# A two-block transformer kernel: unit matrices added by VectorE in an RWKV scan, a store waited for later, and branch gates computed beside memory attention

## The chip, the core and the metric

The kernel is one program for one core of one Trainium2 chip. TensorE (PE) multiplies matrices into PSUM; VectorE (DVE), ScalarE (ACT) and GpSimd (POOL) work on tiles of 128 partitions; SyncE (SP) issues the transfers. Each engine takes its instructions in the order in which they are written, and engines wait for one another by semaphores. The metric is the device time of one execution in microseconds (us).

## The reference

The first block has an attention layer and a recurrent layer, the second a mixer of three branches between two feed-forward layers. Two parts matter here. In the recurrent layer, an RWKV scan goes forwards and backwards over 256 context and 512 latent tokens, eight heads of 64:

```python
def wkv_scan(s0, r, decay, k, v, kk, b, reverse, emit):
    def step(s, inp):
        r_t, w_t, k_t, v_t, kk_t, b_t = inp
        sa = jnp.einsum('bhij,bhj->bhi', s, kk_t)
        s = s * w_t[:, :, None, :] - sa[..., None] * b_t[:, :, None, :] + v_t[..., None] * k_t[:, :, None, :]
        y = jnp.einsum('bhij,bhj->bhi', s, r_t) if emit else None
        return s, y
```

In the mixer the three branches are gated and merged:

```python
        o_dn = rms_norm_2(o_dn, dn_out_norm[l]) * jax.nn.silu(dn_z.reshape(b, s, DN_HEADS, DN_HEAD_DIM))
        o_mem = memory_cross_attention(...)
        gates = jax.nn.sigmoid(u @ w_branch_gate[l]).reshape(b, s, N_BRANCH, d)
        merged = (gates[:, :, 0] * (o_nsa @ w_branch_nsa[l])
                  + gates[:, :, 1] * (o_dn @ w_branch_dn[l])
                  + gates[:, :, 2] * (o_mem @ w_branch_mem[l]))
        x = x + rms_norm_2(merged @ w_out[l], mix_post_norm[l])
```

## The kernel before, in words

The program is a chain of stages. A stage has its own tiles and semaphores, and ends when all engines have come to its end and the transfers it waits for have landed. Weights are split into a high and a low part (ACT's cast at L197, DVE's difference at L201), and a product of a 128x512 tile with eight blocks is 24 matmuls (L220 to L222).

`rwkv_features` makes decay, key and query tiles of the scan, in eight units. A unit has four 128x768 tiles for `s_feat` in device memory: two called `out` (buffers in `rec_y` and a feature tile), a rate and a key tile. SP stores them at L1970 once the semaphore `features` says that the whole unit is done, and loads the first group's tiles back (L1977) after unit 6.

`rwkv_scan` takes 64 tokens as one chunk. Twelve groups (n = 0 to 11), two directions in turn, hold two chunks of all eight heads. The state after a chunk needs the inverse of a triangular 64x64 matrix per head and chunk. It is made from diagonal blocks by powers: the inverse of 1 + D is (1 - D)(1 + D^2)(1 + D^4)(1 + D^8) and so on, so `square`, `four` and `eight` are made one from another, each multiplied onto `inv`; then two steps, `upper` (ux) and `halved` (wx), join the halves. The unit matrices in these factors come from PE: `constant` (L2291) multiplies the unit matrix `eye` with `units` or `twice` into PSUM, and the products (`tiles`, L2282) are added there. A matmul of 64 rows uses a quadrant of the array; "crossed" products take their rows and write their columns on different quadrants. The results come out of PSUM in halves: ACT copies one (`half`, L2614), DVE the other (`odd_half`, L2552). DVE also makes `diag_t`, `diag` (L2533, L2538) and the masked grams (L2547), and the state (L2570, L2571); POOL forms the first factor (L2502) and `off_t` (L2506). The scan of group n-1 (`scan_sa` L2428, `scan_new` L2447 and L2452, `scan_out` L2442 and L2468) is written between the steps of group n, by hand; eight groups with n >= 4 have output, added to `rec_scanned` (L2581, L2585).

In the mixer, the 24 gate tiles of 128x512 are u times a weight, scaled by DVE (`rooted`, L3785). Eight (`gates_first`) are made beside the delta scan (`Beside`), twelve (`gates_kept`) in the earlier attention and kept in device memory (`s_gate`), and four in the stage `merge_gates` after memory attention. There, too, the first eight sigmoids (`Opened`, L824) and the norm of the delta branch's output (`NormAside`: square L1203, sums L1185, root L1206, reciprocal L1211, spread L1193, application L1215, then the product at L3940) are placed between its tiles. `merge0`, `merge1`, `merge2` multiply a branch with its weight; DVE multiplies the result with the gate (L3948) and adds. `merge0` also holds the twelve kept tiles' sigmoids. `InPairs` puts a `Beside` product between an attention's pairs.

Of the kernel before, what the change touches and what calls it, by code (L numbers as in the profile page):

```python
# [724 lines left out]
class Beside:  # L725
# [4 lines left out]
    def __init__(self, w, name, x, lo, evict, banks):  # L730
        self.w, self.x, self.lo, self.evict, self.banks = w, x, lo, evict, banks
        self.first, self.end = w.ranges[name]
        self.limit, self.tiles = w.split_limit(name), self.end - self.first

    def begin(self, st):
        self.ps = [st.ps(f"beside{i}", [P, BANK]) for i in range(self.banks)]
        self.product_done, self.stored = st.sem("beside_product_done"), st.sem("beside_stored")
# [27 lines left out]


class InPairs:
# [10 lines left out]
    def sp(self, sp):  # L778
        for n in range(self.product.tiles):
            self.product.load(sp, n)  # L780
            sp.wait_ge(self.product.stored, n + 1)
            self.put(sp, n).then_inc(self.saved, 16)
        sp.wait_ge(self.saved, 16 * self.product.tiles)
# [6 lines left out]
    def act(self, act, i):  # L790
        if i % self.per == 0 and i // self.per < self.product.tiles:
            self.product.high(act, i // self.per)

# [9 lines left out]
class Opened:  # L803
# [4 lines left out]
    def __init__(self, tiles, per, arrived=None):  # L808
        self.tiles, self.per, self.arrived = tiles, per, arrived
# [10 lines left out]
    def act(self, act, n, wait_stored):  # L820
        if n == 0 and self.arrived is not None:
# [1097 lines left out]
def rwkv_features(nc, name, d, c, v, us, vt, v_feat, bonus, ends, spare, loads, up_w, up_a, first_feats):  # L1919
# [7 lines left out]
    with Stage(nc, name) as st:  # L1927
# [16 lines left out]
         gated, gate_done, lifted, rate_gated, rate_done, key_scale, logs, exps, keyed, kept, features, own, first) = (  # L1944
# [3 lines left out]
                 "key_scale", "logs", "exps", "keyed", "kept", "features", "own", "first"))  # L1948
# [14 lines left out]
        def _(sp):  # L1963
            sp.dma_start(sums[:], d["c_sums"]).then_inc(landed, 16)
            for n in range(n_units):
                at = slice((n % 4) * P, (n % 4) * P + P)
                sp.wait_ge(features, n + 1)
                for j, (tile, sem) in enumerate(((out[n % 2][0], saved_out[n % 2]), (out[n % 2][1], saved_out[n % 2]),
                                                 (rates[n % 3], saved_keys[n % 3]), (keys[n % 3], saved_keys[n % 3]))):
                    sp.dma_start(d["s_feat"][n // 4, j, at, :], tile).then_inc(sem, 16)  # L1970
# [10 lines left out]
            for i in range(3):  # L1981
                sp.wait_ge(saved_keys[i], 32 * len(range(i, n_units, 3)))
# [2277 lines left out]
```

## Time and profile before

| | |
|---|---|
| median of 3 runs | 3320.42 us (3320.09 to 3335.84) |
| profiled execution | 3320.01 us, its span 3318.2 us |
| PE busy | 2961.3 us, 89% |
| DVE busy | 1521.4 us, 46% |
| ACT busy | 1090.3 us, 33% |
| POOL busy | 30.2 us, 1% |
| reload of the kept gates, 3072 KB | 11.0 us from issue to landing |

The shares are means over the whole span. A matmul of four-byte data on 64 rows has two records in the trace, so 32 matmuls in the code are 64 records. PEclk is the clock granted to TensorE, 0.50 being 1.2 GHz and 1.00 being 2.4 GHz. Names in a row are those of the tiles, without buffer numbers. The program's last part is the second feed-forward layer, which the change leaves alone.

### The profile page before, as it was taken

The numbers are of one execution on the slowest core, as the hardware profiler recorded it, in microseconds if no ns is written. First come the engines' busy times: TensorE is split into PE (matmuls) and PEld (weight loads), VectorE is DVE, ScalarE is ACT, GpSimd is POOL, SyncE is SP. The second block draws the span as 40 slices with busy tenths as digits, with TensorE's granted clock in tenths as the row PEclk, the third lists the DMA queues.
The fourth block names the chain that finished last, engine by engine and source line by source line (L and its number), as shares of the span: only waits on it lengthen the run. The fifth ranks groups of instructions, "written<-read, shape, count | busy, mean of one in ns | idle before, by whom it ended". The sixth has DMA issues, their size and how long they took to land. (4 is left out here: it accounts for less than half of the span.)

```text
span 3318.2 us, 55284 instructions
## 1 busy us (share of the span) xinstructions
PE 2961.3 (89%) x24050; PEld 2254.6 (68%) x24050; DVE 1521.4 (46%) x2488; ACT 1090.3 (33%) x1929; POOL 30.2 (1%) x28
## 2 busy tenths in 40 slices
PE   7799989989986898887899999799887988899998
PEld 3488766867854777445788787566655866788876
DVE  5623247354545344556454424355446435354522
ACT  5411367232253333212322123355323233332221
POOL 0000000000000010000000000000000000000000
PEclk9899999989968999788999998899888999999998
DMA  7511200123113111111233222421212122222321
GB/s 267 151 58 51 49 1 2 51 76 127 33 74 126 42 42 42 35 64 51 64 95 95 86 88 65 129 67 42 77 51 66 33 77 70 70 77 90 97 86 64
DMA packets 246083, 243.36 MB, mean 73 GB/s; under 512 B 28248, under 2 KB 216152, under 8 KB 245777
## 3 DMA queue, kind: packets, MB, share of 16 engines
q1 hardware_dynamic: 245538, 238.64, 23.1%
q8 instruction: 190, 3.11, 0.4%
q10 hardware_dynamic: 304, 1.18, 0.1%
q14 instruction: 51, 0.42, 0.0%
HBM read 217.03 MB, written 22.24 MB: 72 GB/s over the span
## 5 line engine op out<-in xcount | busy, mean ns | idle before, releaser
L201 DVE TENSOR_TENSOR second_w_low<-second_w_raw,second_w_high 128x1024 fp32r<-128x1024 f32 (+1 forms) x228 | 272.4, 1197 | 483.0 <-ACT second_w_high L197 482.4
L197 ACT CAST second_w_high<-second_w_raw 128x1024 fp32r<-128x1024 f32 (+1 forms) x228 | 233.0, 1024 | 689.5 <-PE ffn_in_acc L222 250.9
L220 PE MATMUL ffn_in_acc<-ffn_h_high,second_w_high 128*128 128x512 f32 x704 | 281.1, 399 | 13.9 <-DVE ffn_h_low L578 13.9
L222 PE MATMUL ffn_in_acc<-ffn_h_high,second_w_low 128*128 128x512 f32 x704 | 283.0, 402 | 0.0
L221 PE MATMUL ffn_in_acc<-ffn_h_low,second_w_high 128*128 128x512 f32 x704 | 279.7, 397 | 0.0
L201 DVE TENSOR_TENSOR first_w_low<-first_w_raw,first_w_high 128x1024 fp32r<-128x1024 f32 x115 | 140.1, 1222 | 266.4 <-ACT first_w_high L197 265.7
L197 ACT CAST first_w_high<-first_w_raw 128x1024 fp32r<-128x1024 f32 x115 | 120.2, 1047 | 233.2 <-PE attn_in_acc L222 80.9
L220 PEld LDWEIGHTS ffn_in_acc<-ffn_h_high,second_w_high 128*128 128x128 f32 x704 | 133.5, 190 | 47.8 <-issue 17.1
L220 PE MATMUL attn_in_acc<-attn_h_high,first_w_high 128*128 128x256 f32 (+1 forms) x416 | 144.3, 347 | 14.4 <-DVE attn_h_low L323 14.4
L221 PEld LDWEIGHTS ffn_in_acc<-ffn_h_low,second_w_high 128*128 128x128 f32 x704 | 133.7, 190 | 34.2 <-issue 0.5
L222 PEld LDWEIGHTS ffn_in_acc<-ffn_h_high,second_w_low 128*128 128x128 f32 x704 | 133.6, 190 | 31.1
L220 PE MATMUL ffn_down_acc<-ffn_mid_high,second_w_high 128*128 128x512 f32 x352 | 141.9, 403 | 5.9 <-PEq L43 5.9
L221 PE MATMUL attn_in_acc<-attn_h_low,first_w_high 128*128 128x256 f32 (+1 forms) x416 | 142.6, 343 | 0.0
L222 PE MATMUL attn_in_acc<-attn_h_high,first_w_low 128*128 128x256 f32 (+1 forms) x416 | 142.5, 342 | 0.0
L222 PE MATMUL ffn_down_acc<-ffn_mid_high,second_w_low 128*128 128x512 f32 x352 | 140.1, 398 | 0.0
L221 PE MATMUL ffn_down_acc<-ffn_mid_low,second_w_high 128*128 128x512 f32 x352 | 139.8, 397 | 0.0
L220 PEld LDWEIGHTS attn_in_acc<-attn_h_high,first_w_high 128*128 128x128 f32 x416 | 79.4, 191 | 30.1 <-issue 15.9
L221 PEld LDWEIGHTS attn_in_acc<-attn_h_low,first_w_high 128*128 128x128 f32 x416 | 79.7, 192 | 9.7 <-issue 0.2
L222 PEld LDWEIGHTS attn_in_acc<-attn_h_high,first_w_low 128*128 128x128 f32 x416 | 79.5, 191 | 9.8
L220 PEld LDWEIGHTS ffn_down_acc<-ffn_mid_high,second_w_high 128*128 128x128 f32 x352 | 67.0, 190 | 22.2 <-issue 6.7
L222 PEld LDWEIGHTS ffn_down_acc<-ffn_mid_high,second_w_low 128*128 128x128 f32 x352 | 66.9, 190 | 16.9
L220 PE MATMUL rwkv_in_acc<-rec_h_high,first_w_high 128*128 128x512 f32 (+1 forms) x208 | 71.3, 343 | 7.2 <-PEq L43 7.2
(801 smaller groups left out, 6378.3 us busy)
## 6 DMA issues: line engine op xcount, KB each, us to landing
second_w_raw<-in_ffn_w_gate SPq DMA_DIRECT2D x44, 512.0 KB, 3.6
second_w_raw<-in_ffn_w_up SPq DMA_DIRECT2D x44, 512.0 KB, 3.6
second_w_raw<-in_ffn_w_down SPq DMA_DIRECT2D x40, 512.0 KB, 3.4
first_w_raw<-in_rec_w_in SPq DMA_DIRECT2D x33, 512.0 KB, 3.8
first_w_raw<-in_attn_ada_w SPq DMA_DIRECT2D x24, 512.0 KB, 4.7
first_w_raw<-in_rec_ada_w SPq DMA_DIRECT2D x24, 512.0 KB, 5.1
second_w_raw<-in_w_in SPq DMA_DIRECT2D x24, 512.0 KB, 3.7
second_w_raw<-in_w_branch_gate SPq DMA_DIRECT2D x24, 512.0 KB, 3.9
```

Source lines behind the costliest of these rows:

```text
L197: act.copy(self.view(self.high[b % self.splits], b), self.view(self.raw[b % self.bufs], b)).then_inc(self.high_done, 1)
L201: dve.tensor_tensor(self.view(self.low[b % self.splits], b), self.view(self.raw[b % self.bufs], b), self.view(self.high[b % self.splits], ...
L220: pe.matmul(out, sh, mh, start=(first and j == 0), stop=False)
L221: pe.matmul(out, sh, ml, start=False, stop=False)
L222: ins = pe.matmul(out, sl, mh, start=False, stop=(last and j == len(parts) - 1))
```

## The change

1. Scan. `constant` is gone. `square`'s products and the last factor's are on crossed quadrants like the rest, which needs `diag_crossed`: eight more matmuls in the early gram, and a DVE operation. DVE's `with_units` brings both halves out of PSUM and adds `units` or the new `lower` as it does. ACT's halves are gone. POOL's first factor is in two parts, and POOL clears `rec_scanned`, which DVE did. PE's first gram no longer waits for DVE.
2. Features. `out` tiles are stored when they stand (`outs`), and the last unit's rate and key stores are waited for in the scan (`last_saved`).
3. Gates. `merge_gates` is gone. Its four tiles are made beside memory attention; sigmoid becomes 0.5 (1 + tanh) with 0.5 in the scale before and in the copy after `mix_out`; the tanh of the first eight is in the delta scan, the norm in `merge0`, the tanh of kept tiles in `merge0` (from its tile 4) and `merge1`.

```diff
-        for tile in self.tiles[n * self.per:(n + 1) * self.per]:
-            act.activation(tile, tile, ACT.Sigmoid).then_inc(self.opened, 1)
+        for tile in self.tiles[(n - self.first) * self.per:(n - self.first + 1) * self.per]:
+            act.activation(tile, tile, ACT.Tanh).then_inc(self.opened, 1)
...
+                sp.wait_ge(outs, n + 1)
+                for j in range(2):
+                    sp.dma_start(d["s_feat"][n // 4, j, at, :], out[n % 2][j]).then_inc(saved_out[n % 2], 16)
                 sp.wait_ge(features, n + 1)
-                for j, (tile, sem) in enumerate(((out[n % 2][0], saved_out[n % 2]), (out[n % 2][1], saved_out[n % 2]),
-                                                 (rates[n % 3], saved_keys[n % 3]), (keys[n % 3], saved_keys[n % 3]))):
-                    sp.dma_start(d["s_feat"][n // 4, j, at, :], tile).then_inc(sem, 16)
+                for j, tile in ((2, rates[n % 3]), (3, keys[n % 3])):
+                    sp.dma_start(d["s_feat"][n // 4, j, at, :], tile
+                                 ).then_inc(saved_keys[n % 3] if n + 1 < n_units else last_saved, 16)
...
+                else:
+                    sp.wait_ge(last_saved, 32)
...
             def square(n):
                 if n:
-                    pe.wait_ge(act_done, RWKV_ACT(n - 1, "way"))
-                constant(late, 0, all_of(units), 0)
-
-                def products():
-                    pe.wait_ge(dve_done, RWKV_DVE(n, "diag"))
-                    for h in range(2):
-                        tiles(late, 0, dt, dn, 0, 0, (h,), False)
-                        tiles(late, 256, dn, dt, 0, 0, (h,), False).then_inc(pe_done, 1)
-                return products
+                    pe.wait_ge(act_done, RWKV_ACT(n - 1, "solved"))
+                pe.wait_ge(dve_done, RWKV_DVE(n, "diag"))
+                tiles(late, 0, dt, dn, 0, 1)
+                tiles(late, 256, dn, dt, 0, 1).then_inc(pe_done, 1)
...
+                pe.wait_ge(dve_done, RWKV_DVE(n, "square1"))
+                tiles(early, 0, a2[:, 1], a2[:, 0], 1, 0)
+                tiles(early, 256, a2[:, 0], a2[:, 1], 1, 0).then_inc(pe_done, 1)
+                pe.wait_ge(pool_done, RWKV_POOL(n, "first1"))
+                tiles(late, 0, a2[:, 1], m, 1, 0).then_inc(pe_done, 1)
...
             def sixteen(n):
                 pe.wait_ge(dve_done, RWKV_DVE(n, "eight"))
-                constant(early, 0, all_of(units))
                 pe.wait_ge(act_done, RWKV_ACT(n, "m2"))
-                tiles(late, 0, a8, m, 0, 0).then_inc(pe_done, 1)
...
-                constant(sa_ps, 256, wide(twice[:, 0]))
...
+            pool.memset(y[:], 0.0).then_inc(zeroed, 1)
             for n in range(last + 1):
                 dr = groups[n][0]
+                each = eye.rearrange("p (a t) -> p a t", a=1).broadcast_to([P, PAIRS, CH])
                 pool.wait_ge(dve_done, RWKV_DVE(n, "diag"))
-                pool.tensor_tensor(all_of(m).rearrange("p (a t) -> p a t", t=CH),
-                                   eye.rearrange("p (a t) -> p a t", a=1).broadcast_to([P, 2 * PAIRS, CH]),
-                                   all_of(dn).rearrange("p (a t) -> p a t", t=CH), ALU.subtract).then_inc(pool_done, 1)
+                pool.tensor_tensor(m[:, 0], each, dn[:, 0], ALU.subtract).then_inc(pool_done, 1)
...
-            dve.memset(state[:], 0.0).then_inc(cleared, 1)
-            dve.memset(y[:], 0.0).then_inc(cleared, 1)
+            for dr in range(2):
+                dve.tensor_tensor(near[:, dr, :], chunk[:, 2 * dr, :], same, ALU.mult)
...
+                of = bank(out_ps, 1)[:, 256:512].rearrange("p (i t) -> p i t", t=CH)
+                dve.tensor_tensor(crossed[:], of, mask(1 - dr), ALU.mult).then_inc(dve_done, 1)
...
-            def odd_half(n, name, to, ps):
+            def with_units(n, name, to, ps, of=units):
                 dve.wait_ge(pe_done, RWKV_PE(n, name))
-                dve.tensor_copy(to[:, :, 1].rearrange("p a i t -> p a (i t)"),
-                                bank(ps, 1).rearrange("p (a t) -> p a t", a=2)).then_inc(dve_done, 1)
+                for h in range(2):
+                    dve.tensor_tensor(to[:, :, h].rearrange("p a i t -> p a (i t)"),
+                                      bank(ps, h).rearrange("p (a t) -> p a t", a=2),
+                                      of.rearrange("p a i t -> p a (i t)"), ALU.add).then_inc(dve_done, 1)
...
+                    with_units(n, "square", a2, late)
...
-                    odd_half(n, "ux", ux, early)
-                    odd_half(n, "wx", wx, sa_ps)
+                    with_units(n, "ux", ux, early)
+                    with_units(n, "wx", wx, sa_ps, lower)
...
+                    if n:
+                        beside.treat(act, n - 1)
+                beside.treat(act, 7)
...
+            attention(nc, "mem", pairs, [dict(out=branch[2][:, :, t * P:(t + 1) * P]) for t in range(4)], c["ident"], dims=P,
+                      beside=InPairs(Beside(w, "gates_last", *u, lambda e, n, ps: rooted(e, last_tile(n), ps, 0.5), 1, last_tile), 2))
...
-            linear(nc, "merge_gates", w, *u, S, lambda e, n, ps: rooted(e, gate(done + n), ps), engines="v",
-                   then=lambda n: lambda act: act.activation(gate(done + n), gate(done + n), ACT.Sigmoid),
...
+            norm_out = NormAside(c, "dn_out", [branch[1][:, i, :] for i in range(4)], [v("dn_out_norm")] * 4,
+                                 c["pick_mean128"], spread[0:4, :], rs[0:4, :], [out[:, 5, :], out[:, 6, :]], normed,
+                                 dict(square=lambda i: i // 2, sum=lambda i: 1 + i // 2, root=3, inverse=3, apply=lambda i: 5 + i // 2),
+                                 finish=lambda dve, i: dve.tensor_tensor(branch[1][:, i, :], branch[1][:, i, :],
+                                                                         zg[:, i, :], ALU.mult))
+            asides = [Asides(norm_out, Opened([gate(GATES_FIRST + i) for i in range(8)], 2, kept, 4)),
+                      Asides(Opened([gate(GATES_FIRST + i) for i in range(8, GATES_KEPT)], 2)), None]
...
-                ins = dve.tensor_tensor(g, g, ps[:, 0:S], ALU.mult)
+                ins = dve.scalar_tensor_tensor(out=g, in0=g, scalar=1.0, in1=ps[:, 0:S], op0=ALU.add, op1=ALU.mult)
```

PE's queue in the scan, from the early gram of group 1 (`rwkv_early`, `rwkv_out`) to the first product of the fours, before:

```order
L2306 MATMUL rwkv_early<-rwkv_feat 64x128 x16
L2324 MATMUL rwkv_out<-rwkv_feat 64x64 x16
L2291 MATMUL rwkv_late<-rwkv_units,rec_chunk 64x512 x4
L2282 MATMUL rwkv_late<-rwkv_diag,rwkv_diag_t 64x64 x8
L2282 MATMUL rwkv_late<-rwkv_diag_t,rwkv_diag 64x64 x8
L2282 MATMUL rwkv_late<-rwkv_diag,rwkv_diag_t 64x64 x8
L2282 MATMUL rwkv_late<-rwkv_diag_t,rwkv_diag 64x64 x8
L2428 MATMUL rwkv_sa<-rwkv_state,rwkv_way 64x64 x8
L2291 MATMUL rwkv_early<-rwkv_twice,rec_chunk 64x256 x4
L2282 MATMUL rwkv_early<-rwkv_square 64x64 x32
```

and after:

```order
L2312 MATMUL rwkv_early<-rwkv_feat 64x128 x16
L2328 MATMUL rwkv_out<-rwkv_feat 64x64 x16
L2333 MATMUL rwkv_out<-rwkv_feat 64x64 x8
L2297 MATMUL rwkv_late<-rwkv_diag,rwkv_diag_t 64x64 x16
L2297 MATMUL rwkv_late<-rwkv_diag_t,rwkv_diag 64x64 x16
L2426 MATMUL rwkv_sa<-rwkv_state,rwkv_way 64x64 x8
L2297 MATMUL rwkv_early<-rwkv_square 64x64 x32
```

The constants are out, the squares are two sets instead of four, and a set of eight is added to the gram.

DVE's queue in the scan, from `upper` of one group to `four` of the next, before:

```order
L2552 COPY rwkv_upper<-rwkv_early 128x2x256
L2552 COPY rwkv_halved<-rwkv_sa 128x2x256
L2547 TENSOR_TENSOR rwkv_gram_k<-rwkv_early,rec_chunk 128x512 x2
L2533 TENSOR_TENSOR rwkv_diag_t<-rwkv_early,rwkv_near 128x256 x2
L2538 TENSOR_TENSOR rwkv_diag<-rwkv_out,rwkv_near 128x256 x2
L2547 TENSOR_TENSOR rwkv_gram_b<-rwkv_early,rec_chunk 128x512 x2
L2563 TENSOR_TENSOR rwkv_minus_sa<-rwkv_solved,rwkv_sa 64x512
L2552 COPY rwkv_four<-rwkv_early 128x2x256
```

and after:

```order
L2555 TENSOR_TENSOR rwkv_upper<-rwkv_early,rwkv_units 128x2x256 x2
L2555 TENSOR_TENSOR rwkv_halved<-rwkv_sa,rwkv_lower 128x2x256 x2
L2549 TENSOR_TENSOR rwkv_gram_k<-rwkv_early,rec_chunk 128x512 x2
L2533 TENSOR_TENSOR rwkv_diag_t<-rwkv_early,rwkv_near 128x256 x2
L2538 TENSOR_TENSOR rwkv_diag<-rwkv_out,rwkv_near 128x256 x2
L2541 TENSOR_TENSOR rwkv_diag_crossed<-rwkv_out,rwkv_near 128x256
L2549 TENSOR_TENSOR rwkv_gram_b<-rwkv_early,rec_chunk 128x512 x2
L2555 TENSOR_TENSOR rwkv_square<-rwkv_late,rwkv_units 128x2x256 x2
L2567 TENSOR_TENSOR rwkv_minus_sa<-rwkv_solved,rwkv_sa 64x512
L2555 TENSOR_TENSOR rwkv_four<-rwkv_early,rwkv_lower 128x2x256 x2
```

The square is a new pair of operations behind `gram_b`, `upper`, `halved` and `four` are pairs where they were one, and `diag_crossed` stands behind `diag`.

DVE's queue at the end of `merge0`, from the last split but one of a weight tile, after:

```order
L201 TENSOR_TENSOR second_w_low<-second_w_raw,second_w_high 128x1024
L3952 SCALAR_TENSOR_TENSOR memory_gates_first<-memory_gates_first,merge_acc 128x512 x2
L1225 SCALAR_TENSOR_TENSOR mix_branch<-mix_branch,vectors,merge_dn_out_spread 128x512
L3942 TENSOR_TENSOR mix_branch<-mix_branch,mix_dn_z 128x512
L1225 SCALAR_TENSOR_TENSOR mix_branch<-mix_branch,vectors,merge_dn_out_spread 128x512
L3942 TENSOR_TENSOR mix_branch<-mix_branch,mix_dn_z 128x512
L201 TENSOR_TENSOR second_w_low<-second_w_raw,second_w_high 128x1024
L3952 SCALAR_TENSOR_TENSOR memory_gates_first<-memory_gates_first,merge_acc 128x512 x2
L1225 SCALAR_TENSOR_TENSOR mix_branch<-mix_branch,vectors,merge_dn_out_spread 128x512
L3942 TENSOR_TENSOR mix_branch<-mix_branch,mix_dn_z 128x512
L1225 SCALAR_TENSOR_TENSOR mix_branch<-mix_branch,vectors,merge_dn_out_spread 128x512
L3942 TENSOR_TENSOR mix_branch<-mix_branch,mix_dn_z 128x512
```

Before, the applications stood behind the evictions of `merge_gates`:

```order
L201 TENSOR_TENSOR second_w_low<-second_w_raw,second_w_high 128x1024 x2
L3785 TENSOR_TENSOR mix_branch_gates<-merge_gates_acc,mix_root 128x512 x2
L1215 SCALAR_TENSOR_TENSOR mix_branch<-mix_branch,vectors,merge_gates_dn_out_spread 128x512
L3940 TENSOR_TENSOR mix_branch<-mix_branch,mix_dn_z 128x512
L1215 SCALAR_TENSOR_TENSOR mix_branch<-mix_branch,vectors,merge_gates_dn_out_spread 128x512
L3940 TENSOR_TENSOR mix_branch<-mix_branch,mix_dn_z 128x512
L1215 SCALAR_TENSOR_TENSOR mix_branch<-mix_branch,vectors,merge_gates_dn_out_spread 128x512
L3940 TENSOR_TENSOR mix_branch<-mix_branch,mix_dn_z 128x512
L1215 SCALAR_TENSOR_TENSOR mix_branch<-mix_branch,vectors,merge_gates_dn_out_spread 128x512
L3940 TENSOR_TENSOR mix_branch<-mix_branch,mix_dn_z 128x512
```

Two applications and their products now follow the last two evictions of `merge0`.

## Rows read from the trace of the kernel before

**Rows 1.** Windows of five stretches; columns after the length: busy us and instructions, clock, DMA.
```profile
1034.30:1318.30 284.00, 254.77 (x8920) 215.32 (x8924) 115.34 (x214) 96.77 (x171) 27.49 (x22) 0.99 0.15 42
2691.30:2714.83 23.53, 20.75 (x144) 18.14 (x144) 10.94 (x28) 15.36 (x52) 0.00 (x0) 1.00 0.00 1
2714.83:2758.40 43.57, 33.48 (x112) 19.92 (x112) 16.26 (x18) 17.36 (x24) 0.00 (x0) 0.92 0.36 121
2759.90:2765.10 5.20, 5.20 (x12) 4.09 (x13) 2.88 (x4) 3.72 (x7) 0.00 (x0) 0.50 0.48 160
2765.10:2785.88 20.78, 19.76 (x85) 15.66 (x83) 9.18 (x11) 7.35 (x12) 0.00 (x0) 1.00 0.18 59
```

**Rows 2.** Waits of PE in the scan: us in total, times, longest.
```profile
PE rwkv_late L2282 <- ACT rwkv_value L2647: 6.8, 10, 0.7
```

**Rows 3.** Timeline: start us, us, engine, line, instruction; end of features, start of scan.
```profile
1020.97 0.96 DVE L2190 TENSOR_TENSOR rec_y<-rec_y,rwkv_feat_growth 128x768 f32<-128x768 f32 x1
...
1022.80 1.71 SPq L1970 DMA_DIRECT2D s_feat<-rec_y  x2
1030.45 2.23 SPq L2270 DMA_DIRECT2D rwkv_feat<-s_feat  x4
...
1033.17 0.23 DVE L2515 TENSOR_SCALAR rwkv_units<-rec_chunk 128x256 f32<-128x256 f32 x1
...
1034.32 1.98 PE L2306 MATMUL rwkv_early<-rec_first_feats 64*64 64x128 f32 x32 [27.79 <-DVE rwkv_near L2520]
...
1036.44 0.75 DVE L2533 TENSOR_TENSOR rwkv_diag_t<-rwkv_early,rwkv_near 128x256 f32<-128x256 f32 x2 [2.18 <-PE rwkv_early L2306]
```

**Rows 4.** Windows of one us each before and after the last stores of the features.
```profile
1014.00:1015.00 1.00, 0.00 (x0) 0.00 (x0) 0.97 (x2) 0.00 (x0) 0.00 (x0) 0.50 0.00 0
1027.00:1028.00 1.00, 0.00 (x0) 0.00 (x0) 0.00 (x0) 0.00 (x0) 0.00 (x0) 0.50 0.62 249
```

**Rows 5.** Timeline: the squares of one group of the scan.
```profile
1160.57 1.89 PE L2291 MATMUL rwkv_late<-rwkv_units,rec_chunk 64*64 64x512 f32 x8
1161.03 0.74 DVE L2538 TENSOR_TENSOR rwkv_diag<-rwkv_out,rwkv_near 128x256 f32<-128x256 f32 x2
1161.69 1.27 DVE L2547 TENSOR_TENSOR rwkv_gram_b<-rwkv_early,rec_chunk 128x512 f32<-128x512 f32 x2
...
1162.29 0.63 PE L2282 MATMUL rwkv_late<-rwkv_diag,rwkv_diag_t 64*64 64x64 f32 x16
...
1164.37 0.59 ACT L2614 COPY rwkv_square<-rwkv_late 128x512 f32<-128x512 f32 x1 [0.35 <-PE rwkv_late L2282]
...
1165.02 1.16 PE L2282 MATMUL rwkv_early<-rwkv_square 64*64 64x64 f32 x64
```

**Rows 6.** Timeline: the last factor, in an earlier group without output.
```profile
1143.87 1.09 PE L2291 MATMUL rwkv_early<-rwkv_units,rec_chunk 64*64 64x512 f32 x8
1144.00 0.68 DVE L2563 TENSOR_TENSOR rwkv_minus_sa<-rwkv_solved,rwkv_sa 64x512 f32<-64x512 f32 x1 [0.18 <-PE rwkv_sa L2428]
...
1145.63 0.28 PE L2282 MATMUL rwkv_late<-rwkv_inv,rwkv_eight 64*64 64x64 f32 x3
```

**Rows 7.** Timeline: the `halved` copy in one group, the last output addition in another.
```profile
1152.16 0.69 DVE L2552 COPY rwkv_halved<-rwkv_sa 128x512 f32<-128x512 f32 x1 [1.89 <-PE rwkv_sa L2282]
...
1176.58 0.85 DVE L2585 TENSOR_TENSOR rec_scanned<-rec_scanned,rwkv_out 64x256 f32<-64x256 f32 x2
```

**Rows 8.** Timeline: norm, end of `merge_gates`, first matmuls of `merge0` and `merge1`.
```profile
2736.49 1.88 PE L1185 MATMUL merge_gates_dn_out_sums<-residual,constants 128*4 128x512 f32 x4 [3.00 <-ACT residual L1203]
...
2756.66 0.74 DVE L1215 SCALAR_TENSOR_TENSOR mix_branch<-mix_branch,vectors,erge_gates_dn_out_spread 128x512 f32<-128x512 f32 x1
...
2759.89 0.76 PE L220 MATMUL merge_acc<-mix_branch_now_high,second_w_high 128*128 128x512 f32 x1 [3.33 <-DVE mix_branch_now_low L299]
...
2787.36 0.47 PE L220 MATMUL merge_acc<-mix_branch_now_high,second_w_high 128*128 128x512 f32 x1 [2.50 <-DVE mix_branch_now_low L299]
```

**Rows 9.** Timeline of POOL: its first operation in the scan.
```profile
1038.06 1.27 POOL L2502 TENSOR_TENSOR rwkv_inv<-rec_chunk,rwkv_diag 128x512 f32<-128x512 f32 x1 [1037.61 <-DVE rwkv_diag L2538]
```

More of the change, by code:

```diff
@@ L792, in act @@
             self.product.high(act, i // self.per)
+        if i % self.per == 0 and 1 <= i // self.per <= self.product.tiles and self.product.opened is not None:
+            self.product.treat(act, i // self.per - 1)
     def dve_first(self, dve, i):
@@ L806, with __init__ @@
     banks = 0
-    def __init__(self, tiles, per, arrived=None):
-        self.tiles, self.per, self.arrived = tiles, per, arrived
+    def __init__(self, tiles, per, arrived=None, first=0):
+        self.tiles, self.per, self.arrived, self.first = tiles, per, arrived, first
     def begin(self, st, followed):
@@ L1943, in rwkv_features @@
         (cleared, landed, tanhed, constant, v_turned, v_stored, squared, scaled, summed, rooted, inverted, spread, turned, normed,
-         gated, gate_done, lifted, rate_gated, rate_done, key_scale, logs, exps, keyed, kept, features, own, first) = (
+         gated, gate_done, lifted, rate_gated, rate_done, key_scale, logs, exps, keyed, kept, features, own, first, outs) = (
              st.sem(x) for x in (
@@ L2274, in _, with tiles @@
         def _(pe):
-            def tiles(ps, first, lhs, rhs, crossed, to_crossed, heads=(0, 1), start=True):
+            def tiles(ps, first, lhs, rhs, crossed, to_crossed, heads=(0, 1)):
                 for i in range(PAIRS):
@@ L2340, in four @@
+                pe.wait_ge(dve_done, RWKV_DVE(n, "diag"))
+                tiles(late, 0, dt, dn, 0, 1)
+                tiles(late, 256, dn, dt, 0, 1).then_inc(pe_done, 1)
             def four(n):
                 pe.wait_ge(dve_done, RWKV_DVE(n, "gram1"))
-                constant(early, 256, wide(twice[:, 0]))
-                def products():
-                    pe.wait_ge(act_done, RWKV_ACT(n, "square1"))
-                    tiles(early, 0, a2[:, 1], a2[:, 0], 0, 1, start=False)
-                    tiles(early, 256, a2[:, 0], a2[:, 1], 0, 1, start=False).then_inc(pe_done, 1)
-                    pe.wait_ge(pool_done, RWKV_POOL(n, "first"))
-                    tiles(late, 0, a2[:, 1], m, 0, 1).then_inc(pe_done, 1)
@@ L2596, in _ @@
                 if n <= last:
-                    odd_half(n, "four", a4, early)
+                    with_units(n, "four", a4, early, lower)
                 if n:
@@ L2622, in _ @@
                 dr = groups[n][0]
-                for h in range(2):
-                    act.wait_ge(pe_done, RWKV_PE(n, f"square{h}"))
-                    half(n, "square", a2, late, h)
-                act.wait_ge(pe_done, RWKV_PE(n, "four"))
-                half(n, "four", a4, early, 0)
                 whole(n, "step4", m, late)
@@ L3920, in mixer @@
                      for t in range(4) for g in (0, 2)]
-            attention(nc, "mem", pairs, [dict(out=branch[2][:, :, t * P:(t + 1) * P]) for t in range(4)], c["ident"], dims=P)
+            attention(nc, "mem", pairs, [dict(out=branch[2][:, :, t * P:(t + 1) * P]) for t in range(4)], c["ident"], dims=P,
+                      beside=InPairs(Beside(w, "gates_last", *u, lambda e, n, ps: rooted(e, last_tile(n), ps, 0.5), 1, last_tile), 2))
         attended.close()
```

144 lines of the change are left out of this document (72 added, 72 removed).

## The prediction

> **What bounds the kernel now.** I read the table of busy shares first: TensorE (PE) 89%, VectorE (DVE) 46%, ScalarE (ACT) 33%. The change touches three stretches, so the windows come next [rows 1]. In 284 us of the scan, eleven of its twelve groups (25.8 us each), PE is busy for 254.77 us and DVE for 115.34, 41%; of the releasers that PE waits for most, the waits list gives only 6.8 us in ten times [rows 2]. So the scan is PE's queue, in order, and an instruction less on PE counts as far as its place was not under a wait for something else. In memory attention PE is busy for 20.75 of 23.53 us. The `merge_gates` stage takes 43.57 us from the end of memory attention to the first operation of `merge0`, with 33.48 us of PE in it. Third comes the timeline, for what ends each wait: at the end of the features DVE ends at 1021.93, the last stores are issued by 1024.5, and the scan begins only at 1030.45 [rows 3]; there no engine works, and the DMAs set the time.
>
> The sum is made against the profiled execution, 3320.0 us (its span 3318.2 and 1.8 around it), 0.4 below the median of the runs.
>
> **Stores of the features and the start of the scan.** Before, SP stores all four tiles of a unit when the last is done, and the stage waits for all. The transfers ran out in the microsecond after 1027 (share 0.62) [rows 4], 2.4 us ahead of the scan's first instruction. Now the two `out` tiles of a unit go as soon as they stand, and the last two key tiles, 768 KB, are waited for by SP in the scan, before its first load, which group 1 needs some 25 us later. The last-but-one unit's `out` stores fall into the time when nothing moved (share 0.00 at 1014) [rows 4]; the last byte waited for is then some 5 us earlier, 1023. With the same 2.4 us the scan starts at 1025.5: **-5.0**. Bounds: -2.4 if only the keys' 768 KB leave (at 249/0.62 = 400 GB/s, near 2 us, and the end of it), -7.7 if DVE's end at 1021.93 and a gap of about 1 us set it.
> In the scan before, PE's first gram waited for DVE's whole preparation (a 128x2048 memset in it), and began at 1034.32; `diag_t` followed at 1036.44, 5.8 us after DVE's first operation at 1030.6 [rows 3]. Now PE starts at once and its gram takes 2.0 us; DVE's preparation without the long memset is ten small operations of about 0.23 us (as the one at 1033.17 [rows 3]), 2.3 us. `diag_t` comes at +2.4: **-3.4**. The memset goes to POOL, whose 128x512 operation takes 1.27 us [rows 9]; by that up to 5.1 us (estimate by elements), and POOL's first real operation is wanted at about +4, group 0's product with it at +8: hidden. Bounds: -1 (POOL late by all of that) and -3.6.
>
> **The scan's groups.** PE order shows the late constants of 4x512, the `twice` of 4x256 before the fours, the `units` before the last factor and the `twice` before `halved` gone, eight rows of each in the trace per group. DVE adds unit matrices in its evictions instead, both halves, where ACT took one and DVE the other. Step by step:
> Square. `diag` ended at 1161.77, the constants kept PE until 1162.46, products from 1162.29, ACT's second half done at 1164.96, fours at 1165.02 [rows 5]. Now the products start at 1161.8 and are done by 1163, but DVE's pair stands behind `diag_crossed` (half of 0.74) and `gram_b` (1.27 the pair): 1161.77 + 0.35 + 1.25 + 1.3 = 1164.65. **-0.36**. Here DVE is the new bound, and the products' gain of 0.7 is lost in it.
> Four, upper. A pair of DVE additions is 1.3 (by `gram_b`'s pair), against 0.69 for the one copy that stood beside ACT's: +0.6, with other matmuls of PE in between. In a group with output (n = 5 to 11, seven) 64 scan matmuls hide the four's, in the other four groups only 32: I take 0 and +0.24. For `upper` it is the turns that hide it, except where the output addition keeps DVE until 1177.43 [rows 7]: +0.3 with output, +0.05 without. Each lies between 0 and 0.6.
> Last factor. The constants took PE from 1143.87, the 32 products after them ended at 1145.91, and 0.3 before that the next step began [rows 6]: 1.73. With crossed quadrants the 64 matmuls at 1165.02 all begin within 0.94 (1.16 less the 0.2 that one lasts [rows 5]), 0.47 for 32: 1.3 less. Without output DVE's `minus_sa` until 1144.68 [rows 6] is late next, and 0.84 is left; with output, 16 matmuls more stand between: -1.3.
> Halved. Nothing of PE but the second gram stands beside it. The copy at 1152.16 took 0.69 [rows 7], the pair 1.3, less the head start: **+0.54** in each group.
> Eight more gram matmuls: 0.13 us on PE, under DVE's `diag`. `gram_k` behind the longer `halved` is not wanted before z.
> A group without output: -0.36 + 0.24 - 0.84 + 0.05 + 0.54 = -0.37; with: -0.36 - 1.3 + 0.3 + 0.54 = -0.82; group 0 as the square and the factor alone, -0.45. Sum: 4 x -0.37, 7 x -0.82, -0.45 = **-7.7**. Bounds: all products gained and DVE's pairs hidden, -1.1 a group, -13; only DVE's costs and nothing gained, +0.9 a group, +11.
>
> **Gates.** The stage of 43.57 us goes [rows 1]; its start gap of 0.45 stays with the next: -43.1. What it held comes back elsewhere:
> Its 96 matmuls go beside memory attention. At full clock one takes 19.76/85 = 0.233 us [rows 1]: 22.4. Memory attention's PE idles for 2.8 us, of which I let 1.2 be filled; the last tanh of the delta scan stands at its end, 0.75; one output buffer in place of two, 1.0. **+23.0**. ACT has 15.36 of 23.53 us, and the longer stage has room for its four weight casts and tanh: bounds +20 and +26.
> The norm of the delta branch moves to `merge0`: its sums and spreads, four of these steps of 1.88 [rows 8], are 7.6 us on PE (before they were in the 43.57), with no wait for ACT's squares since these come one step ahead (the two waits of 3.0 us before the sums go with the old stage): **+7.6**. The last two applications and products stand behind the last evictions on DVE, four operations of 0.74 and 0.69 (rows from 2756.66 [rows 8]), after which `merge1` casts: **+2.9**. Before they were alike at the end of the removed stage.
> Clock. `merge0` began after 3.33 us without matmuls [rows 8], and for its first 5.20 us PE was granted 0.50, the 1.2 GHz level: 12 matmuls of 0.433 [rows 1], 2.4 us dearer than at 0.233. `merge1` began after 2.50 us, and at full clock. Now the tail makes that gap 5.4 us: **+2.4**.
> The reload of the kept gates (3072 KB, 11 us to landing, in the table) is wanted by ACT only at tile 4, half of `merge0` or some 15 us in: nothing; if it were late, `merge0` would wait for the difference. All 24 sigmoids become tanh; those of the first eight go under the delta scan's matmuls, but for the last.
> Sum: -43.1 + 23.0 + 7.6 + 2.9 + 2.4 = **-7.2**, bounds -12 and -2.
>
> Total: -5.0 - 3.4 - 7.7 - 7.2 = -23.3, so 3296.7 profiled and **3297** as a median.
>
> **Rivals.**
> *The constants were under waits.* If DVE's `diag` and evictions set each step, their going gives nothing, and DVE's pairs cost 0.54 + 0.3 + the four's: +0.85 a group, +10. Then 3320.4 + 10 - 8.4 - 7.2 = 3315. For: the square's gain is half gone that way already. Against: `diag` was ready 0.5 us ahead of the products [rows 5].
> *The clock holds.* `merge0` and `merge1` both at 2.4 GHz, 4.8 less, and the features bounded by DVE's end, 2.7 less: 3289. For: one gap of 2.50 did not slow. Against: 3.33 did.
> *POOL holds DVE.* If POOL's long memset and DVE's unit copies exclude each other, DVE's preparation stands until +5, then 2 us: `diag_t` at +7 and not +2.4, so +1.2 for -3.4: 3301. Before, no POOL operation ran beside such copies, so no row tells. The Trainium skill, "SBUF — State Buffer", section "Who interferes with whom", has such a rule: copies and tensor_scalar in two-port modes share a port pair with GpSimd, and the one that comes second is fully blocked. That no trace here shows; by that page the time is this rival's 3301.
> *DVE becomes the scan's bound (slower).* Each group gives DVE 0.37 + 1.3 + 3 x 0.62 = 3.5 us more. If all of it stands on the chain, because DVE's queue is entered late at each step, the scan is 12 x 3.5 = 42 longer: 3320.4 + 42 - 8.4 - 7.2 = 3347. It decides from 1.3 us a group: below that, the sum stays under the time before. Against: DVE's share would be 55% of the scan, and PE's own waits for it are small.
>
> **Chances.** Forecast 0.45 (its own range 3289 to 3305), clock 0.15, POOL 0.12, constants under waits 0.20, DVE bound 0.05, something else 0.03. A measurement can tell 0.5%, 16.6 us, from no change: below 3303.8 is faster. Of the forecast 0.39 lies there, all of the clock's, 0.10 of POOL's and 0.02 of the constants': faster 0.66. Slower 0.05; between, 0.29. Range 3284 to 3315: it takes in all but the slower case and half of the constants'.
>
> **What would show it.** The first `diag_t` of the scan 8.4 us earlier in the trace; the interval from a group's early gram to the next 25.2 rather than 25.8; `square` additions starting right behind `gram_b`, with fours 0.1 behind them; PE's idle time before `z` longer by 0.5. Memory attention 46.5 us long, `merge0` 38. Wrong I am if a group is over 26 us, if PE idles for DVE before the fours by more than 1 us, or if memory attention takes over 50 us.

## The result, and the profile after

The changed kernel takes 3338.45 us (median of 12 executions, 3324.3 to 3342.7), the one before 3325.65 us (12, 3316.19 to 3335.84): a ratio of 1.0034, interval 1.002 to 1.0048, 11 us more. 3297 was predicted, range 3284 to 3315. Executions of one kernel lie up to 20 us apart here, so stages are compared in the traces and totals by ratios.

Against the profiled execution of before (3320.01 us), that of after (3339.31 us) stands so, each stretch from its first to its last instruction:

| stretch | predicted | measured |
|---|---|---|
| DVE's end of the features to the scan's first operation | -5.0 | 8.7 to 5.4: -3.3 |
| from there to the first `diag_t` | -3.4 | 5.8 to 3.8: -2.0 |
| first `diag_t` to the twelfth (eleven groups) | -7 | 288.2 to 312.7: +24.6 |
| last state of the delta scan to `mix_out` (154.7 us) | -7.2 | +2.4 |

The rest is -2.3 from the twelfth `diag_t` to the first matmul of the stage after the scan, and what passes between two executions: -1.1 before the features, +6 in one feed-forward stage and -6 behind `mix_out`.

The window of 240 us in the scan, before and after (the granted clock is the third number from the end, 1.00 and 0.96):

```profile
1060.00:1300.00 240.00, 216.13 (x7591) 182.74 (x7591) 100.05 (x187) 82.71 (x146) 24.99 (x20) 1.00 0.16 43
1060.00:1300.00 240.00, 176.47 (x6926) 160.88 (x6927) 120.15 (x222) 52.52 (x92) 22.02 (x25) 0.96 0.15 41
```

From the first `diag_t` to the twelfth it is 0.99 before and 0.94 after.

The timeline of after at the scan's start answers to [rows 3]:

```profile
1020.89 0.82 SPq L1982 DMA_DIRECT2D s_feat<-rec_y  x2
...
1026.26 0.36 DVE L2514 TENSOR_TENSOR rwkv_near<-rec_chunk 128x64 f32<-128x64 f32 x2 [5.39 <-PEq L38]
...
1026.53 1.96 DVE L2515 TENSOR_SCALAR rwkv_units<-rec_chunk 128x256 f32<-128x256 f32 x1
1026.54 1.80 POOL L2497 MEMSET rec_scanned<- 128x2048 f32 x1 [1026.10 <-POOLq L38]
...
1028.41 0.27 DVE L2516 COPY rwkv_units<-rec_chunk 128x256 f32<-128x256 f32 x1
...
1030.08 0.76 DVE L2533 TENSOR_TENSOR rwkv_diag_t<-rwkv_early,rwkv_near 128x256 f32<-128x256 f32 x2
```

PE and DVE begin at 1026.26, together. But one unit copy on DVE takes 1.96 us where it took 0.23, and it ends, at 1028.49, just behind POOL's memset (1026.54 + 1.80 = 1028.34). The next, of the same size, takes 0.27. The windows answering to [rows 4] (DMA share last but one, GB/s last):

```profile
1023.00:1024.00 1.00, 0.00 (x0) 0.00 (x0) 0.00 (x0) 0.00 (x0) 0.00 (x0) 0.50 0.99 399
1024.00:1025.00 1.00, 0.00 (x0) 0.00 (x0) 0.00 (x0) 0.00 (x0) 0.00 (x0) 0.50 0.69 277
1025.00:1026.00 1.00, 0.00 (x0) 0.00 (x0) 0.00 (x0) 0.00 (x0) 0.00 (x0) 0.50 0.14 55
```

The transfers run on to 1025. The key stores, no longer waited for, are issued at 1020.89, so they share the DMA engines with what is; which of the transfers ended last these windows don't tell.

Waits of PE in the scan of after; before, [rows 2] was the largest with a named releaser:

```profile
PE rwkv_early L2297 <- DVE rwkv_square L2555: 13.2, 12, 1.7
PE rwkv_late L2297 <- DVE rwkv_diag L2538: 11.1, 11, 1.6
PE rwkv_early L2297 <- issue: 10.6, 7, 3.0
PE rwkv_late L2297 <- ACT rwkv_value L2640: 8.2, 12, 0.7
PE rwkv_late L2369 <- issue: 7.1, 5, 1.8
```

DVE is waited for at the squares twice in each group. And "issue", idle time of PE for which the trace shows no releaser, sums over all lines of the scan's timeline to 38.4 us in 36 places, where it was 21.5 in 25. A group of after in its timeline, answering to [rows 5], and its end:

```profile
1167.00 1.28 DVE L2555 TENSOR_TENSOR rwkv_square<-rwkv_late,rwkv_units 128x512 f32<-128x512 f32 x2
1168.43 1.27 PE L2297 MATMUL rwkv_early<-rwkv_square 64*64 64x64 f32 x63 [1.10 <-DVE rwkv_square L2555]
...
1185.47 0.55 PE L2312 MATMUL rwkv_early<-rwkv_feat 64*64 64x128 f32 x11 [1.77 <-issue]
...
1186.99 1.11 PE L2303 MATMUL rwkv_sa<-constants,rwkv_feat 128*128 128x128 f32 x4
...
1188.03 1.98 PE L2399 MATMUL rwkv_sa<-rec_v_tokens,rwkv_gram_k 64*64 64x64 f32 x32
...
1219.11 1.15 PE L2399 MATMUL rwkv_sa<-rec_v_tokens,rwkv_gram_k 64*64 64x64 f32 x32
```

The fours begin 0.15 behind the end of DVE's `square` pair (0.1 was predicted), after 1.10 us without matmuls. At 1185.47 PE begins again after 1.77 us of "issue", and then goes at half the clock: the granted clock in the four microseconds from 1186 is 0.63, and the product at L2399 takes 1.98 us, in the next group 1.15. Five of the seven slow stretches of the clock between the first and the twelfth `diag_t` begin just behind a stop of 1.7 to 3.0 us by "issue". The other two follow waits for DVE: the longest, from about 1033 to 1048, begins in group 0's waits of 1.60 and 1.65 us for `diag` and `square`, and one stands behind 0.94 us for `diag` at 1138.

### The profile page after: what moved, and what is told of

Same layout as the page of the kernel before. It is cut to its first block and busy times, and to the rows that moved or that the text cites. A ratio compares the mean times of both kernels' runs of the same rounds, so it can differ in the third digit from the quotient of the medians.

```text
span 3337.5 us, 54950 instructions
## 1 busy us (share of the span) xinstructions
PE 2934.3 (88%) x23858; PEld 2249.3 (67%) x23858; DVE 1561.3 (47%) x2561; ACT 1054.9 (32%) x1868; POOL 34.3 (1%) x41
```

## The experiments

**The three parts one by one.** e1_scan has part 1 of the change, e2_store part 2, e3b_gates part 3, each on the kernel before.

```diff
# e1_scan: rwkv_scan and its Marks as changed, but without
-                else:
-                    sp.wait_ge(last_saved, 32)
# e2_store: rwkv_features as changed, and in rwkv_scan of before only
+                else:
+                    sp.wait_ge(last_saved, 32)
# e3b_gates: Beside, InPairs, Opened, delta_branch and mixer as changed
```

> Part 1 (scan) alone; stores and gates as before. The whole change lost 22 us between the scan's first diag_t and its end, with 12 waits of PE for the square's additions (13.2 us), 11 for diag (11.1) and PE idle without a releaser for 38.4 us where it was 21.5. Theory S (the loss is the scan's own): this kernel is 12 to 22 us slower than before, with the same waits. Rival (the loss comes with the stores' or gates' part, or is noise between executions, whose times here spread over 16 us): within 5 us of before.

> Part 2 (stores of the features) alone, scan and gates as before. In the whole change the scan's first operation came 3.1 us earlier against the end of the features' matmuls, for 5.0 predicted. Theory: it is DVE's end plus the stage's change that bounds now; -3 us here. Rival: nothing, since the key stores delay the first loads of the scan: 0.

> Part 3 (gates) alone, scan and stores as before. In the whole change this stretch, memory attention to mix_out, was 2.4 us longer, with -7.2 predicted: memory attention has two waits of 2.05 us for DVE's gate eviction and a slow stretch of clock behind one of them, merge0 is 3.7 us over the sum with a granted clock of 0.84, 0.73 and 0.69 in its last third. Theory: these stand here too, +2 us. Rival: they came from the whole change's other moment in the clock; then -3 to -7.

e1_scan: ratio 1.005 (1.0038 to 1.0062), +16.6 us; first to twelfth `diag_t` 308.1 us; idle without releaser 40.2 us. Theory S holds. e2_store: 0.9983 (0.9971 to 0.9995), -5.6 us (-1.6 to -9.6); in its trace the scan begins 5.5 us behind DVE's end for 8.7, the -3 of the theory. e3b_gates: 0.9994 (0.9982 to 1.0006), no difference to be told; its trace has both waits of 2.05 us and is 2.3 us longer than before from the delta scan to `mix_out`, as theory and whole change had it. The three sum to +9, and the whole lost 11: they add up within the intervals, and the loss is in the scan. Between scans whose groups are those of before, the eleven groups took 288.2 us (before), 290.9 (e3b_gates), 293.7 (e2_store) and 295.4 (e7_start, below), so differences under some 7 us between two scans mean nothing. Before's is the shortest: of the +24.6 in the table some 4 are its luck, against the mean of these four it is +20.6.

**The constants issued again.** e4_fill is e1_scan with them, as products that nobody reads. The constants are those of before in number and shape, the first of a group now on crossed quadrants (1.3 us for 1.9 in [rows 5]); the gram's eight more matmuls and DVE's adding are as in the change.

```diff
+            def constant(ps, first, of, crossing=1):
+                for h in range(2):
+                    for j in range(2):
+                        r, n = rows(j ^ (h & crossing)), of.shape[1]
+                        pe.matmul(ps[rows(j), h * BANK + first:h * BANK + first + n], eye[r, :], of[r, :], start=True, stop=True)
...
+                constant(late, 0, all_of(units))
                 pe.wait_ge(dve_done, RWKV_DVE(n, "diag"))
```

(and likewise ahead of the fours, the last factor and the turns; in group 0 PE first waits for DVE's unit tiles)

> e1_scan with the removed constants' matmuls issued again in their old places, into PSUM that the next products overwrite; DVE still adds the unit matrices, and nothing reads what they write. Theory F (without the constants PE idles between short matmuls, and the granted clock falls in the scan; and PE's instruction supply, which long matmuls gave time, falls behind): the scan is 6 us or more shorter than e1's, slow stretches and idle time without a releaser near those of before. Rival D (DVE's added evictions are the whole loss): the scan is as long as e1's or longer, by up to 12 x 1 us, since the last factor's constants stand in the way again.

Ratio 1.0003 (0.9993 to 1.0012): as fast as before, 0.47% or 16 us faster than e1_scan, with more work on TensorE and none less elsewhere. First to twelfth `diag_t` is 292.5 us for 308.1. Waits of PE in e1_scan:

```profile
PE rwkv_early L2282 <- DVE rwkv_square L2540: 13.7, 12, 1.7
PE rwkv_late L2282 <- DVE rwkv_diag L2523: 11.9, 12, 1.3
```

and in e4_fill:

```profile
PE rwkv_early L2282 <- DVE rwkv_square L2552: 6.7, 12, 0.9
```

The waits for `diag` are under the constants, and half of those for the square. But these waits are in DVE's chain and their end doesn't come earlier for it. What fell beside them is the idle time without releaser, 40.2 to 27.1 us, and the clock's slow stretches: in windows of 2 us from the first `diag_t` to the twelfth, those with a clock below 0.97 are 2 for 17 (before 3, after 26). Over the same 240 us, e1_scan and then e4_fill:

```profile
1060.00:1300.00 240.00, 176.88 (x6969) 161.71 (x6963) 121.01 (x224) 52.81 (x93) 24.14 (x27) 0.97 0.14 39
1060.00:1300.00 240.00, 202.64 (x7599) 169.95 (x7599) 126.87 (x235) 56.01 (x99) 24.21 (x27) 1.00 0.16 43
```

Rival D falls: e4_fill has all of DVE's work, and its 292.5 us lie among the unchanged scans. Theory F holds with both of its halves together, supply and clock; this run doesn't part them.

**The same in small pieces.** e5_fill_small issues each constant in pieces of 64 columns.

```diff
-                        pe.matmul(ps[rows(j), h * BANK + first:h * BANK + first + n], eye[r, :], of[r, :], ...)
+                        for a in range(0, n, CH):
+                            at = h * BANK + first + a
+                            pe.matmul(ps[rows(j), at:at + CH], eye[r, :], of[r, a:a + CH], start=True, stop=True)
```

> e4_fill (3327.1 against 3344.8 for the scan's part alone) with each constant in pieces of 64 columns: the same columns through PE, but 4 or 8 times the instructions, 96 a group instead of 16. Theory C (the constants gave PE something to do, and with it the clock): as fast as e4, ratio to before 0.999 to 1.002. Theory I (they gave the instruction supply time, by being few and long): PE's idle time without a releaser rises over e1's 40 us, and the scan is at least as slow as e1's, ratio 1.004 or more.

Ratio 1.0195 (1.0176 to 1.0214), so theory C's number failed; but the idle time without releaser was 27.9 us and not over 40, so theory I's sign failed too. The trace tells why it can't decide:

```profile
1122.77 3.06 PE L2291 MATMUL rwkv_late<-rwkv_units,rec_chunk 64*64 64x64 f32 x59
```

59 short records take PE 3.06 us, busy, where eight long ones took 1.9 [rows 5] and, in e4_fill, 1.3: these pieces, which follow one another on one quadrant, are dear in themselves (64 crossed products began within 0.94 us in before), and with 96 matmuls a group for 16 a group is 5.3 us longer than e4_fill's (350.3 us from the first `diag_t` to the twelfth). It decides neither theory.

**How fast short instructions come.** e8_supply is e2_store with a run of extra matmuls in two groups.

```diff
+                if n == 2:
+                    for _ in range(32):
+                        tiles(early, 0, units, units, 0, 1)
+                if n == 3:
+                    for _ in range(32):
+                        constant(early, 0, all_of(units))
                 constant(early, 256, wide(twice[:, 0]))
```

> e2_store with extra matmuls in the scan, into PSUM that is written anew behind them: ahead of group 2's fours 512 matmuls of 64 columns on crossed quadrants (1024 records), ahead of group 3's fours 128 matmuls of 512 columns (256 records). It measures how fast PE can be given short instructions. In the scan PE's idle times without a releaser stand 99 to 128 records apart, or a multiple of that, and one transfer of instructions is 16.4 KB, 128 records of two instructions of 64 bytes. Theory I (blocks of 128 records come no faster than one in about 4 us): the short ones run 0.015 us apart (1.9 us a block), then stop at each block for some 2 us, 30 us or more for the 1024; the long ones take 0.27 us each without such stops. Rival (the idle times are something else, as a collision with the transfers of features): 1024 records in about 15 us without regular stops.

(3373.73 us in its one execution, 3319.59 for before.)

```profile
1093.97 2.10 PE L2287 MATMUL rwkv_early<-rwkv_units 64*64 64x64 f32 x128 [1.37 <-issue]
1097.44 2.10 PE L2287 MATMUL rwkv_early<-rwkv_units 64*64 64x64 f32 x128 [1.37 <-issue]
1101.18 1.04 PE L2287 MATMUL rwkv_early<-rwkv_units 64*64 64x64 f32 x55 [1.64 <-issue]
...
1144.45 23.76 PE L2296 MATMUL rwkv_early<-rwkv_units,rec_chunk 64*64 64x512 f32 x217
```

The first run is a beat: 128 records in 2.10 us, then 1.37 us of nothing, then 128 more (the eight pauses are 1.0 to 1.9 us). From the stop at 1090.51 to that at 1119.40 there are eight blocks in 28.9 us, 3.6 us each. The long matmuls ran 23.8 us without a stop, 217 records shown of 256. Theory I holds: a block of 128 records (16.4 KB of instructions, one packet of the instruction queue) comes every 3.5 to 4.0 us, and next to nothing else moved on the DMA queues meanwhile (5 GB/s on average), so no collision made the stops. In seven traces of the scan, 209 distances from one stop by "issue" to the next are a multiple of 128 records, within 4, and never shorter than 3.46 us a block. In a stretch of 240 us of before's scan (1060 to 1300), the trace shows 7591 records of matmuls and 59 packets of instructions, a block in 4.07 us; 3.6 is nine tenths of that. But the beat isn't the whole rule. In the changed scan there are fewer packets, 54, a block in 4.4 us, and more stops; and stops one block apart stand 3.5 to 5.9 us apart. What makes a block come later than the beat, by what PE had done before or by other transfers, no run here shows.

**The start without the collision.** e7_start is e2_store with the changed start, and POOL's memset behind group 0's operations.

```diff
+                if n == 0:
+                    pool.memset(y[:], 0.0).then_inc(zeroed, 1)
```

> e2_store with the scan's start of the change, its groups as before: PE's first gram waits for nothing of DVE, DVE makes its small tiles first, and POOL clears rec_scanned, but after its operations for group 0 and not beside DVE's unit copies. Theory (the 1.96 us of one unit copy in the changed kernel, 0.23 before, were the wait for POOL's 1.80 us memset): that copy takes 0.2 to 0.3 us, and the first diag_t stands 2.3 us behind DVE's first operation, 3.8 in the changed kernel and 5.8 before; -3 us against e2. Rival (copies at the start of a stage are slow for another reason, as the first read of a tile): it stays at 1.9 and diag_t at 3.8.

```profile
1022.05 0.36 DVE L2521 TENSOR_TENSOR rwkv_near<-rec_chunk 128x64 f32<-128x64 f32 x2 [4.85 <-PEq L38]
...
1022.33 0.28 DVE L2522 TENSOR_SCALAR rwkv_units<-rec_chunk 128x256 f32<-128x256 f32 x1
...
1024.17 0.76 DVE L2538 TENSOR_TENSOR rwkv_diag_t<-rwkv_early,rwkv_near 128x256 f32<-128x256 f32 x2 [0.41 <-PE rwkv_early L2311]
...
1028.21 1.80 POOL L2514 MEMSET rec_scanned<- 128x2048 f32 x1
```

The copy takes 0.28, `diag_t` comes 2.1 us behind DVE's first operation, for 3.8 in the change and 5.8 before; POOL's memset still takes 1.80, while DVE does nothing. Ratio 0.9981 (0.9968 to 0.9994). Against e2_store's 0.9983 this isn't to be told in the total; in the trace it is.

**The gates without the waits.** e6_gates_low has two edits on e3b_gates.

```diff
+                if beside is not None:
+                    beside.dve_last(dve, i)
                 if i >= 2 and last_of[group[i - 2]] == i - 2:
                     finish(group[i - 2])
-                if beside is not None:
-                    beside.dve_last(dve, i)
...
-  ... root=3, inverse=3, apply=lambda i: 5 + i // 2)
+  ... root=3, inverse=3, apply=lambda i: 4 + i // 2)
```

> e3b with two edits: in attention DVE splits the next weight tile before it finishes a group of outputs, not behind it; in merge0 the norm's applications stand one tile earlier (tiles 4 and 5). Theory: the two waits of 2.05 us and the clock's fall behind one of them go (-4 to -6 in memory attention), and merge0's tail on DVE of 2.9 us goes, with the gap before merge1 3.2 instead of 5.3 us (-3 to -5): 7 to 11 us less than e3b. Rival: the wait for the eviction is set by PE's own product just before, and the clock falls after any gap of 3 us: 2 to 3 us less only.

The wait in e3b_gates:

```profile
2721.82 0.47 PE L220 MATMUL mem_beside<-mix_u_high,second_w_high 128*128 128x512 f32 x1 [2.05 <-DVE memory_gates_last L3799]
...
2753.68 0.76 PE L220 MATMUL merge_acc<-mix_branch_now_high,second_w_high 128*128 128x512 f32 x1 [3.34 <-DVE mix_branch_now_low L299]
...
2795.35 0.77 PE L220 MATMUL merge_acc<-mix_branch_now_high,second_w_high 128*128 128x512 f32 x1 [5.26 <-DVE mix_branch_now_low L299]
```

and in e6_gates_low:

```profile
2710.07 0.48 PE L220 MATMUL mem_beside<-mix_u_high,second_w_high 128*128 128x512 f32 x1 [0.92 <-DVE memory_gates_last L3799]
...
2739.25 0.76 PE L220 MATMUL merge_acc<-mix_branch_now_high,second_w_high 128*128 128x512 f32 x1 [3.34 <-DVE mix_branch_now_low L299]
...
2782.06 0.47 PE L220 MATMUL merge_acc<-mix_branch_now_high,second_w_high 128*128 128x512 f32 x1 [2.51 <-DVE mix_branch_now_low L299]
```

The two waits fall from 2.05 to 0.92 us, and memory attention, from its first score to `merge0`, from 53.5 to 49.6 us. The second edit did half: the gap before `merge1` is 2.51 us, and the clock stays up behind it (0.47 us for the first matmul, 0.77 with the gap of 5.26), but `merge0` is 42.8 us for 41.7. In all 3.6 us less in the trace, under the 7 to 11 of the theory and over the 2 to 3 of the rival; the ratio is 0.9972 (0.9959 to 0.9985) against 0.9994, 7 us, with intervals that touch.

**What paid, together.** e9_both is e7_start with e6_gates_low's gates. 

> The parts that paid, together: e7_start (stores, early start of the scan, POOL's memset behind group 0; ratio 0.9981) and e6_gates_low (gates with the weight split first and the norm a tile earlier; 0.9972); the scan's groups as before, with the constants on TensorE. If the two are independent: 0.995, 3309 us, and so faster than both kernels. Rival: the gains are noise of the single comparisons, 0.998 to 1.0.

Ratio 0.9961 (0.9947 to 0.9975), median 3306.71 us: 13 us below the kernel before, and by the two ratios 24 below the change. It is a little less gain than the two multiplied (0.9953), within the intervals.

## Why the prediction was wrong

**The step that failed is that of the scan's groups**: "So the scan is PE's queue, in order, and an instruction less on PE counts as far as its place was not under a wait for something else." It was to give -7.7 and gave about +18.6 (e1_scan's 16.6, and 2.0 that its start won). What the runs show in its place is that taking out the constants costs time, and issuing them again, unread, gives 15.6 us of the scan back (e4_fill). Two things come back with them.

The first is the supply of instructions. PE's come in blocks of 128 records, at best one in 3.5 us, and PE runs through crossed 64x64 products in 2.1 us a block (e8_supply). The constants were 32 records a group in some 4 us, long and few, during which the next block could come. Without them PE stops for its supply in 36 places for 25, three a group for two, and for longer each time; e4_fill has 13.1 us less of these stops than e1_scan.

The second is the clock, for which the scan's step has no term. Time lost to it can be estimated as the length of each window times what its clock lacks to 1.00: at most 10.3 us in e1_scan and 1.2 in e4_fill, 18.8 in the change and 2.5 before, each from the first `diag_t` to the twelfth. So up to 9 of the 15.6 us can be the clock's, and at least 6 are not. The clock fell mostly behind stops of the supply, but also behind waits for DVE. Group 0 shows its price with the same code, in one trace each: in the change the clock is at half for some 14 us of it and it takes 25.6 us, in e1_scan for 4 us and it takes 22.8. How supply, clock and PE's waits for DVE divide the loss stays open.

The rows that would have told were there: "issue" before many first matmuls of the scan of before, 21.5 us in all, each time a multiple of 128 records apart, within 2. The prediction has no term for them. In the change they stand nearer; these are one block apart each:

```profile
1118.45 0.51 PE L2297 MATMUL rwkv_late<-rwkv_inv,rwkv_four 64*64 64x64 f32 x19 [0.87 <-issue]
...
1123.38 0.28 PE L2369 MATMUL rwkv_late<-rec_chunk,rwkv_inv 64*64 64x64 f32 x3 [1.51 <-issue]
...
1127.89 0.40 PE L2297 MATMUL rwkv_sa<-rwkv_upper 64*64 64x64 f32 x11 [0.76 <-issue]
```

The signs of being wrong that the prediction set all came: a group took 28.4 us (over 26), PE idled 1.10 us for DVE before the fours (over 1), memory attention took 51.5 us (over 50). Within its sum, group 0's term of -0.45 doesn't follow from the square and the factor alone (-0.36 and -0.84); that changes nothing here.

**Square, four, upper, last factor, halved.** The mechanism was read right where DVE comes in: fours 0.15 behind the `square` pair. PE's 1.0 and 1.1 us of waiting for `diag` and `square` in each group cost nothing by themselves (e4_fill has DVE's chain and is as fast as before), but they were time in which PE did nothing, and in group 0 and at 1138 the clock fell behind them.

**Start of the scan.** -3.4 predicted, -2.0 measured. The rival "POOL holds DVE" was right as to mechanism, wrong as to size: the memset takes 1.80 us and not 5.1, so `diag_t` was 1.7 late, not 4.6. Here the Trainium skill's "SBUF — State Buffer", section "Who interferes with whom", and the trace agree: the unit copy took 1.96 us beside the memset and 0.28 without (e7_start).

**Stores.** -5.0 predicted, -3.3 in the trace, and -5.6 by e2_store (-1.6 to -9.6). The transfers ended near 1025 and not at 1023, and the scan began about 1.1 us behind them, where the sum had kept 2.4. That the keys' transfers, going beside, held up those waited for is the likely reason of the first; no run has them apart.

**Gates.** -7.2 predicted, +2.4 in the trace, -2.0 by e3b_gates (-6 to +2). Memory attention was mis-sized by 5.7 us: I gave the single PSUM bank of the product 1 us, and it cost two waits of 2.05 us, since DVE's eviction stood behind a weight split that stood behind the finish of a group, and at the first of the two the clock fell as well. `merge0` was 3.7 us over: the granted clock fell in it once more, behind the spreads. The timeline of after:

```profile
2791.86 1.98 PE L1203 MATMUL merge_dn_out_spread<-residual 4*128 4x512 f32 x4
...
2794.34 0.39 PE L222 MATMUL merge_acc<-mix_branch_now_high,second_w_low 128*128 128x512 f32 x1
...
2794.86 0.63 PE L221 MATMUL merge_acc<-mix_branch_now_low,second_w_high 128*128 128x512 f32 x1
...
2809.86 0.76 PE L220 MATMUL merge_acc<-mix_branch_now_high,second_w_high 128*128 128x512 f32 x1 [5.26 <-DVE mix_branch_now_low L299]
...
2838.16 0.47 PE L220 MATMUL merge_acc<-mix_branch_now_high,second_w_high 128*128 128x512 f32 x1 [3.23 <-DVE mix_branch_now_low L299]
```

The tail (+2.9) and `merge1`'s slow start (+2.4, a gap of 5.26 us) came as predicted, by `merge1`'s 28.3 us for 25.8 before.

**The rivals.** The slower one named DVE as the new bound, with 42 us if all stood on the chain. The sign was right, the cause was not: e4_fill has all of DVE's work and is as fast as before. "Constants under waits" had the idea that their going gives nothing, but no term for its costing. "The clock holds" fell: `merge0` and `merge1` both began at half clock (0.76 us for the first matmul).

## What to carry to other kernels

Look for gaps without a releaser by their distance in instructions, not in time. In a stretch of short matmuls, with such gaps a multiple of 128 records apart and a block of 128 in about 4 us, the queue is held up by its instructions, and a few long instructions taken out give nothing and may cost. Price what an emptier queue does to the clock as well. When a memset is moved to POOL, place it where DVE waits, and not beside its copies (e7_start).

## What the runs showed that was not expected

PE can be slowed by where its instructions come from: 128 records in 2.10 us, then 1.0 to 1.9 us of nothing, eight times over (e8_supply).

The granted clock fell in `merge0` though PE had not been idle: what it had done before was four spreads, 1.98 us with an operand of four partitions, and 1 us behind them the matmuls went from 0.39 to 0.63 us (2.4 to 1.2 GHz). And in the changed kernel `merge2`, after 3.23 us without a matmul, began at full clock (0.47), where `merge0`, after 3.34, began at half (0.76), as it had before the change after 3.33 [rows 8]. Before the change `merge2` too began at half (0.77) after the same 3.23 us: the length of a gap alone doesn't tell what the clock will be.
